# Two attention forms computed by pairs of 64-wide heads, with the values stationary and the output left transposed

## The reference

```python
def one_block(qi):                      # full attention, layers 1 and 2
    s = jnp.einsum("bqgrd,bkgd->bgrqk", qi, k)
    p = jax.nn.softmax(s, axis=-1)
    return jnp.einsum("bgrqk,bkgd->bqgrd", p, v)
...
valid = (jnp.abs(rel) <= WINDOW) & (kpos[:, None, :] >= 0) & (kpos[:, None, :] < S)
scores = jnp.where(valid[None, :, None, None], scores, NEG)   # banded, layers 3 and 4
m = jnp.maximum(jnp.max(scores, axis=-1, keepdims=True), sink_l)
p = jnp.exp(scores - m)
p = p / (jnp.sum(p, axis=-1, keepdims=True) + jnp.exp(sink_l - m))
...
p = jax.nn.softmax(s, axis=-1)          # differential, layers 3 and 4
w = p[:, :, 0] - lam * p[:, :, 1]
...
mixed = jnp.concatenate([attn_out, ssd_out], axis=-1)
x = x + jnp.einsum("ble,ed->bld", mixed, w_out[i])
```

## Time and profile before

| | us |
|---|---|
| median of three runs | 2754.73 |
| the profiled execution, its own time | 2757.43 |
| its span, first to last instruction | 2755.6 |
| TensorE busy, share of the span | 2574.8, 93% |
| VectorE busy | 1522.2, 55% |
| ScalarE busy | 886.4, 32% |
| GpSimd busy | 303.1, 11% |
| mean granted TensorE clock, share of full | 0.956 |

### The profile page before, as it was taken

One profiled execution on the slowest core, in us unless ns is written; L12 is line 12 of the kernel. 1 busy time (PEld: TensorE's weight loads), 2 busy tenths in 40 slices (PEclk: granted clock), 3 DMA queues, 4 the chain that ended last, 5 costly groups with the idle time before them and its releaser, 6 DMA issues.

```text
span 2755.6 us, 31048 instructions
## 1 busy us (share of the span) xinstructions
PE 2574.8 (93%) x12620; PEld 2146.9 (78%) x12620; DVE 1522.2 (55%) x2164; ACT 886.4 (32%) x1284; POOL 303.1 (11%) x205
## 2 busy tenths in 40 slices
PE   7898899999998889999999778999999796999999
PEld 6677788888877778888887667888888585888887
DVE  5755543434575554443467675646465767464645
ACT  4351332223335133222242453322233244322222
POOL 2102200000210120000035101000002600100000
PEclk9999899999999989999999788999999888999999
DMA  4200022222310002222222001222232200132232
GB/s 166 77 16 1 31 97 102 92 96 102 109 63 31 1 31 92 94 105 92 92 95 99 21 1 47 92 94 101 96 107 103 81 1 1 61 107 92 92 107 92
DMA packets 30238, 205.33 MB, mean 75 GB/s; under 512 B 3344, under 2 KB 3728, under 8 KB 6032
## 3 DMA queue, kind: packets, MB, share of 16 engines
q1 hardware_dynamic: 30096, 203.35, 20.8%
HBM read 201.24 MB, written 2.10 MB: 74 GB/s over the span
## 4 chain that ended last, share of the span: by engine, by line
PE 80%; DVE 11%; POOL 3%; ACT 3%; issue 2%; DVEq 1%; ACTq 0%; DMA 0%; SPq 0%; POOLq 0%
PE bank L1304 23%; PE bank L1306 23%; PE bank L1305 23%; PE bank L1416 3%; PE bank L1427 2%; PE bank L1386 1%; POOL b_sqs L1281 1%; POOL head_rs L1285 1%; PE bank L1556 1%; ACT b_p L599 1%; DVE b_p L1157 1%; PE bank L1595 1%; DVE a_conv L867 1%; DVE ssq L698 1%; DVE neg_max L1186 1%
## 5 line engine op out<-in xcount | busy, mean ns | idle before, releaser
L622 DVE TENSOR_TENSOR w_lo<-w_raw,w_hi 128x2048 fp32r<-128x2048 f32 (+1 forms) x190 | 433.9, 2284 | 413.6 <-ACT w_hi L306 413.4
L1304 PE MATMUL bank<-h_ffn_hi,w_hi 128*128 128x512 f32 x1408 | 548.6, 390 | 0.0
L1306 PE MATMUL bank<-h_ffn_hi,w_lo 128*128 128x512 f32 x1408 | 547.8, 389 | 0.0
L1305 PE MATMUL bank<-h_ffn_lo,w_hi 128*128 128x512 f32 x1408 | 547.7, 389 | 0.0
L306 ACT ACTIVATE w_hi<-w_raw 128x2048 fp32r<-128x2048 f32 (+1 forms) x190 | 360.0, 1895 | 558.8 <-PE bank L1306 511.1
L1306 PEld LDWEIGHTS bank<-h_ffn_hi,w_lo 128*128 128x128 f32 x1408 | 264.3, 188 | 55.0
L1305 PEld LDWEIGHTS bank<-h_ffn_lo,w_hi 128*128 128x128 f32 x1408 | 264.3, 188 | 54.8
L1304 PEld LDWEIGHTS bank<-h_ffn_hi,w_hi 128*128 128x128 f32 x1408 | 264.3, 188 | 54.4
L1304 PE MATMUL bank<-act_hi,w_hi 128*128 128x512 f32 x704 | 273.9, 389 | 0.0
L1305 PE MATMUL bank<-act_lo,w_hi 128*128 128x512 f32 x704 | 273.9, 389 | 0.0
L1306 PE MATMUL bank<-act_hi,w_lo 128*128 128x512 f32 x704 | 273.9, 389 | 0.0
(11 more groups left out here) (292 smaller groups left out, 3716.0 us busy)
## 6 DMA issues: line engine op xcount, KB each, us to landing
w_raw<-weights SPq DMA_DIRECT2D x188, 1024.0 KB, 4.7
residual<-x_in SPq DMA_DIRECT2D x8, 256.0 KB, 6.2
x_out<-residual SPq DMA_DIRECT2D x8, 256.0 KB, 2.1
cst<-consts SPq DMA_DIRECT2D x1, 960.0 KB, 10.7
par_b<-params_b SPq DMA_DIRECT2D x1, 627.0 KB, 11.7
par_a<-params_a SPq DMA_DIRECT2D x1, 244.0 KB, 2.7
w_raw<-weights SPq DMA_DIRECT2D x2, 64.0 KB, 1.9
```

The lines of the kernel that those rows point to most:

```text
L622: nc.vector.tensor_tensor(w_lo[s][:, cols], w_raw[s][:, cols], w_hi[s][:, cols].bitcast(F32), ALU.subtract).then_inc(w_ready, 1)
L1304: mm(out, ahi, bhi, start=start, stop=False)
L1305: mm(out, ahi, blo, start=False, stop=False)
L1306: return mm(out, alo, bhi, start=False, stop=stop)
```

## The change

Heads are taken by twos. A key tile is no longer copied into two half-empty ones: head 2j uses rows 0 to 63 of query and key tile and head 2j + 1 rows 64 to 127, each with its own bank (`S_BANKS`). The masks of the banded part come behind the scores and only for the outer blocks. The turned probabilities stream while 64 columns of v are stationary, one head giving partitions 0 to 63 and the other 64 to 127 of bank 4, so that the output is transposed. The reciprocals of the sums are spread over the partitions by eight small products (bank 3), copied, multiplied in (`normalise`), and the result is split where it lies (`out_hi`, `out_lo`): no transposes for these four tiles, which `w_out` takes first, with the turns of the other four behind its first twelve matmuls. Transposes follow the scores two units later instead of one, and VectorE takes the maxima of a differential unit ahead of the weights of the one before. SyncE, GpSimd and the DMAs have the same instructions. Parts of the diff:

```diff
-            def key_hi(m, base, dst):
-                act.wait_ge(t_done, base + m + 1)
-                for half in range(2):
-                    last = nc.scalar.activation(dst[:, key_tile(m, half), :], bank[5 + m % 2][:, :], ACT.Identity,
-                                                scale=half_mask[:, half:half + 1])
-                last.then_inc(t_hi_done, 1)
...
+            def pair_exp(lay, i, par_, width, probs):
+                act.wait_ge(max_done, 32 * lay + 2 * i + par_ + 1)
                 if i >= 2:
+                    act.wait_ge(pt_done, 32 * lay + 2 * (i - 2) + par_ + 1)
+                c = 2 * i + par_
+                nc.scalar.activation(probs[i % 2][par_][:, 0:width], bank[S_BANKS[i % 2][par_]][:, 0:width], ACT.Exp,
+                                     bias=neg_max[:, c:c + 1], accum_out=denom[:, c:c + 1]).then_inc(e_done, 1)
...
+            def normalise(lay, t, r_sb, on):
+                dve.wait_ge(r_taken, 4 * lay + t + 1)
+                dve.wait_ge(o_done, 32 * lay + 8 * t + 8)
+                nc.vector.tensor_tensor(on[:, :], bank[4][:, :], r_sb[:, :], ALU.mult).then_inc(o_free, 1)
+            def out_lo(lay, t, on, hi, lo):
+                dve.wait_ge(o_hi_done, 4 * lay + t + 1)
+                ts_ = slice(t * P, (t + 1) * P)
+                nc.vector.tensor_tensor(lo[:, :, ts_], on[:, :].rearrange("p (j q) -> p j q", q=P), hi[:, :, ts_].bitcast(F32),
+                                        ALU.subtract).then_inc(o_ready, 1)
...
+                    for par_ in range(2):
+                        c = 2 * i + par_
+                        dve.wait_ge(s_done, base + c + 1)
+                        nc.vector.tensor_reduce(neg_max[:, c:c + 1], bank[S_BANKS[i % 2][par_]][:, 0:window(i // 4)[1] * P],
+                                                AX.X, ALU.max, negate=True)
                     dve.drain()
-                    nc.vector.tensor_scalar(neg_max[:, i:i + 1], recip[:, i:i + 1], par[:, B_SINK + h:B_SINK + h + 1], -1.0,
-                                            ALU.max, ALU.mult).then_inc(max_done, 1)
+                    j = i % 4
+                    nc.vector.tensor_tensor(neg_max[:, 2 * i:2 * i + 2], neg_max[:, 2 * i:2 * i + 2], neg_sink[:, 2 * j:2 * j + 2],
+                                            ALU.min).then_inc(max_done, 2)
...
-                for i in range(16 + 4):
+                for i in range(20):
+                    if i < 16:
+                        diff_max(i)
+                    if i == 0:
+                        out_lo(lay, 3, B["b_on"], B["b_ot_hi"], B["b_ot_lo"])
                     if 1 <= i <= 16:
-                        diff_weights(i - 1)
-                    if i < 16:
-                        for c in range(2):
-                            dve.wait_ge(ds_done, 32 * l + 2 * i + c + 1)
-                            nc.vector.tensor_reduce(neg_max[:, 2 * i + c:2 * i + c + 1], bank[(5, 6, 1, 2)[2 * (i % 2) + c]][:, :],
-                                                    AX.X, ALU.max, negate=True).then_inc(dmax_done, 1)
-                    if i >= 7 and (i - 3) % 4 == 0:
-                        t = (i - 3) // 4 - 1
+                        diff_coef(i - 1)
+                    if i >= 7 and i % 4 == 3:
+                        t = (i - 7) // 4
                         take_diff(t)
                         if t >= 1:
...
+            def pair_attention(lay, windows, q_of, k_of, v_of, masked, probs, pts, between):
+                base = 32 * lay
+                def blocks(u):
+                    return window(u // 4) if windows else (0, TB)
+                for i in range(19):
                     if i in between:
                         between[i]()
+                    if i < 16:
+                        t, j = divmod(i, 4)
+                        k0, nb = blocks(i)
                         if i >= 2:
+                            pe.wait_ge(e_done, base + 2 * (i - 2) + 2)
                         qs, ks = slice(t * P, (t + 1) * P), slice(k0 * P, (k0 + nb) * P)
+                        qh, ql = q_of(j)
+                        for n in range(3):
+                            for par_ in range(2):
+                                rows = slice(par_ * HD, (par_ + 1) * HD)
+                                kh, kl = k_of((j // 2) ^ par_)
+                                q_, k_ = ((qh, kh), (qh, kl), (ql, kh))[n]
+                                last = mm(bank[S_BANKS[i % 2][par_]][:, 0:nb * P], q_[rows, qs], k_[rows, ks],
+                                          start=(n == 0), stop=(n == 2 and not masked))
+                                if n == 2 and not masked:
+                                    last.then_inc(s_done, 1)
+                        if masked:
+                            for par_ in range(2):
+                                outer = [b for b in range(nb) if k0 + b != t]
+                                for b in outer:
+                                    last = mm(bank[S_BANKS[i % 2][par_]][:, b * P:(b + 1) * P], id_bf[:, :], mask_bf[:, k0 + b - t + 1, :],
+                                              start=False, stop=(b == outer[-1]))
+                                last.then_inc(s_done, 1)
+                    if 2 <= i < 18:
+                        u = i - 2
+                        nb = blocks(u)[1]
+                        for par_ in range(2):
+                            pe.wait_ge(e_done, base + 2 * u + par_ + 1)
+                            if u >= 1:
+                                pe.wait_ge(ptc[par_], 16 * lay + u)
+                            for b in range(nb):
+                                last = nc.tensor.transpose(bank[PT_BANKS[par_]][:, b * P:(b + 1) * P],
+                                                           probs[u % 2][par_][:, b * P:(b + 1) * P], ident)
+                            last.then_inc(pt_done, 1)
+                    if i >= 5 and i % 4 == 1:
+                        t = (i - 5) // 4
+                        pe.wait_ge(recip_ready, 4 * lay + t + 1)
+                        if t >= 1:
+                            pe.wait_ge(r_taken, 4 * lay + t)
+                        for j in range(4):
+                            for par_ in range(2):
+                                c = 8 * t + 2 * j + par_
+                                last = mm(bank[3][par_ * HD:(par_ + 1) * HD, j * P:(j + 1) * P],
+                                          recip[:, c:c + 1].to_broadcast([P, HD]), ident, start=True, stop=True)
+                        last.then_inc(r_done, 1)
                     if i >= 3:
+                        u = i - 3
+                        t, j = divmod(u, 4)
+                        k0, nb = blocks(u)
+                        if j == 0 and t >= 1:
+                            pe.wait_ge(o_free, 4 * lay + t)
+                        for par_ in range(2):
+                            pe.wait_ge(ptc[par_], 16 * lay + u + 1)
                         for b in range(nb):
+                            for par_ in range(2):
+                                last = mm(bank[4][par_ * HD:(par_ + 1) * HD, j * P:(j + 1) * P], v_of(j // 2, k0 + b),
+                                          pts[u % 2][par_][:, b * P:(b + 1) * P], start=(b == 0), stop=(b == nb - 1))
+                                if b == nb - 1:
+                                    last.then_inc(o_done, 1)
...
-            def w_out(g0, base, n):
+            def w_out(lay, g0, base, n, ot_hi, ot_lo, src):
                 for g in range(g0, g0 + QUARTERS):
                     enter(g)
                     for half in range(2):
                         j = 2 * (g % 2) + half
                         open_bank(j, g)
+                        if g == g0 and half == 0:
+                            pe.wait_ge(o_ready, 4 * lay + 4)
                         for k in range(KT):
-                            if g == g0 and half == 0:
-                                pe.wait_ge(t_free, base + n + k + 1)
+                            if g == g0 and half == 0 and k == 4:
+                                pe.wait_ge(mix_ready, lay + 1)
+                                for m in range(4):
+                                    turn(n + m, base, lambda t: src[:, t, m * P:(m + 1) * P])
+                            if g == g0 and half == 0 and k >= 4:
+                                pe.wait_ge(t_free, base + n + k - 4 + 1)
                             ws = slice(k * COLS + half * P, k * COLS + half * P + P)
-                            last = three(bank[j][:, :], w_hi[g % 2][:, ws], w_lo[g % 2][:, ws], h_mix_hi[:, k, :], h_mix_lo[:, k, :],
+                            hi, lo = (ot_hi, ot_lo) if k < 4 else (h_mix_hi, h_mix_lo)
+                            last = three(bank[j][:, :], w_hi[g % 2][:, ws], w_lo[g % 2][:, ws], hi[:, k, :], lo[:, k, :],
                                          k == 0, k == KT - 1)
...
-                for m in range(8):
-                    if m == 4:
-                        pe.wait_ge(mix_ready, lay + 1)
```

(58 more changed lines are left out.)

345 lines of the change are left out of this document (156 added, 189 removed).

## The result

| | before | after |
|---|---|---|
| median of four runs each, us | 2753.61 | 2665.05 |
| range of the runs | 2751.8 to 2761.34 | 2662.83 to 2666.91 |
| span of the profiled execution | 2755.6 | 2661.0 |
| mean granted TensorE clock | 0.956 | 0.968 |

The ratio is 0.967, 95% interval 0.965 to 0.969: faster by 88.6 us in the medians, 94.6 in the profiled spans. The forecast was 66 less (2688.5); the direction was right and the result lies inside the range of 2655 to 2748, in its lower part.

A forecast was written before the change was run, and what follows sets the result against it. TensorE was taken to bound the kernel, except VectorE's waits in the differential part. Two layers at -18.6 and two at -14.6 gave -66 us: 2691 from the profile's 2757.4, 2688.5 from the median; range 2655 to 2748.

The forecast's parts named there:

- Column halves, x = 0.055: Value and reciprocal products: x, the price of one column-half instruction, is 0.055 us, two halves going side by side.
- Rival A: Column-half products: the halves take turns, x = 0.108 us an instruction, +58 us, 2746 in all; chance 0.17.
- rival C: Column-half products: a load waits for the neighbour's streaming, 0.185 us an instruction, +141 us, 2830 in all; chance 0.10.
- The turn, 0.15 each: TensorE in attention pairs: each change of tiling mode costs 0.15 us, three changes a pair.
- less the 0.07 for how the loads fall: Full-attention pair: 0.07 us taken off for how loads fall, bringing the pair from 3.17 to 3.10 us.
- Full attention, -11.4: Full-attention stage: 16 pairs save 13.8 us, less 1.4 at the end and 1 for a later start; -11.4 us a layer.
- The +1.4 at the end: End of full attention: product, ScalarE rounding and VectorE subtraction now stand before the coefficients; +1.4 us.
- Rival B: Attention loops: the handing over between engines binds, 3.5 us a pair instead of 3.1, +26 us, 2714 in all; chance 0.16.
- Banded part, 0: Banded part: pairs at 2.42 us (two blocks) and 3.06 (three), +2.1 - 1.8 over eight of each, so nothing.
- Differential part, -6: Differential part: VectorE's wait for the exponentials is covered, less time given back to TensorE and its low clock; -6 us a layer.
- Output projection, -6 in all four: Output projection: 12 early matmuls -2.8, mixing ending sooner and four turns -2.6, fewer low-clock matmuls -0.6; -6 us a layer.
- Keys, -1.2: Key turns: two copies a turned tile become one on each engine, two tiles; -1.2 us a layer.

The follow-up runs named there:

- the run with short streams: Changed kernel with every value product except the first block's streaming 64 columns instead of 128; 2654.69 us, ratio 0.964.
- the two runs above: Changed kernel, differential part: VectorE's old order alone put back, 2694.03 us (0.978); TensorE's old order alone put back, 2706.89 us (0.983).
- the version with three edits: Changed kernel with differential takings spread, 24 projection matmuls before the mixing wait, full attention's last subtraction behind the first state products; 2646.81 us, ratio 0.961.

## Why the prediction was right

**Column halves, x = 0.055: right.** 0.0575 by the reciprocals, and (1.03 - 0.15) / 16 = 0.055 by the values. Rival A (0.108) and rival C (0.185) fall. The forecast leaned on row halves going in pairs; the run with short streams shows that streaming two at a time sets the pace. That the loads of two column halves overlap is in the trace itself: the sixteen of a pair's values, 0.14 us each, stand within 0.85 us.

```profile
185.06 0.85 PEld L1489 LDWEIGHTS bank<-a_pt,a_v 128*64 128x64 f32 x16 [0.17 <-issue]
```

The rule that stood behind rival C, that a load overlaps only where the row group differs (the Trainium skill, TensorE: Matmul & The Clock Gate, Part 3), would by rival C's estimate of 0.185 have made a pair's values 3 us; the trace disagrees, with 1.03.

**The turn, 0.15 each: right** (0.15 to 0.17). The "less the 0.07 for how the loads fall" was wrong: without it the pair would have come to 3.17, and 3.16 was measured. By the Trainium skill (TensorEngine Tiling (Array Packing), Key Properties) a change of mode drains the engine; the pair of 3.30 instead of 2.95 us in the run with two more turns agrees.

**Full attention, -11.4: nearly right**, -12.2. Two terms erred and offset each other: the pairs gave 16 x 0.80 = 12.8 instead of 13.8, and the start and the interruptions, priced at +1, cost 0.8 less than before. The +1.4 at the end was there, as moving the subtraction showed. Rival B fell: pairs start every 2.95 us without a gap, and no handing over binds the loop.

**Banded part, 0: wrong, -4.3 beyond the entry.** The step that failed is "scores are held by their loads, two of 128 columns a pass at 0.105 each". A two-block and a three-block pair:

```profile
1534.23 0.39 PE L1446 MATMUL bank<-b_kt_hi,h_mix_hi 64*128 64x256 f32 x2
1534.45 0.28 PE L1446 MATMUL bank<-b_kt_lo,h_mix_hi 64*128 64x256 f32 x2
1534.57 0.28 PE L1446 MATMUL bank<-b_kt_hi,h_mix_lo 64*128 64x256 f32 x2
1534.78 0.29 PE L1454 MATMUL bank<-mask_bf,id_bf 128*128 128x128 bf16 x2
1534.90 0.61 PE L1465 MATMUL bank<-cst,b_p 128*128 128x128 f32 x4
```

```profile
1517.44 0.44 PE L1446 MATMUL bank<-b_kt_hi,h_mix_hi 64*128 64x384 f32 x2
...
1518.52 0.84 PE L1465 MATMUL bank<-cst,b_p 128*128 128x128 f32 x6
1519.29 0.88 PE L1489 MATMUL bank<-b_pt,b_va 128*64 128x128 f32 x12
1520.10 0.44 PE L1446 MATMUL bank<-b_kt_hi,h_mix_hi 64*128 64x384 f32 x2
```

The third pass of both heads starts 0.12 after the second, not 0.21 (1534.45 to 1534.57): the loads of two row halves share time as their streams do. The trace has both loads of the third pass in the same 0.19 us (from 1534.45 on). The first pass, behind a change of mode, takes 0.22. Two-block scores with their turn are 0.55, not 0.82, and two masks 0.12, not 0.20. Summed with values at 0.58 and reciprocals at 0.23 a two-block pair is 2.0 (priced 2.42), a three-block one 2.66 + 0.23 = 2.9 (priced 3.06): 8 x 0.42 + 8 x 0.17 = 4.7.

**Differential part, -6: the mechanism right, the size off**, -8.7 and -9.0. The wait of the reciprocal for the exponentials is gone. VectorE's work alone is 2.4 us a unit (2.48 was priced); up to the first taking such units alternate with some of 2.6 to 2.9 (2.62 in the rows below), behind it not, where "two units in 5.14, 2.57 each" was priced throughout. The first taking is 2.4 us (1563.61 to 1566.01) and not 2.99, as it has no scaling. "About 1.5 after each of three" takings was there behind two of them, 1.72 and 1.50; behind the third no maxima follow. That the order is the cause, VectorE's and TensorE's alike, the two runs above show.

```profile
1557.41 0.15 DVE L1188 RECIPROCAL recip<-denom 128x2 f32<-128x2 f32 x1
...
1560.03 0.15 DVE L1188 RECIPROCAL recip<-denom 128x2 f32<-128x2 f32 x1
...
1562.43 0.15 DVE L1188 RECIPROCAL recip<-denom 128x2 f32<-128x2 f32 x1
```

**Output projection, -6 in all four: right in sum** (-8.8, -7.9, -6.4, -3.6, mean -6.7), too small in layers 1 and 2 and too large in 4. "Fewer matmuls at the low clock, -0.6" was the mis-sized term. In the 30 us from the last y or value product on, the mean granted clock of the four layers was 0.83, 0.77, 0.75 and 0.84 before and is 1.00, 0.94, 0.89 and 0.84 after: in the first layer it doesn't fall at all, in the last it is as low as it was, and the savings fall with the difference. The gap in the middle of the first half, forecast as some 4 us, is 2.6 (1.42 and 1.13) in layer 1 and 3.2 (2.03 and 1.13) in layer 3.

**Keys, -1.2: right in layers 1 and 2, wrong in 3 and 4** (-3.3, -4.3), and the state-space part, not priced, gave 1.5 and 1.9. What goes beyond the price is clock. In layer 1 the first eight state products take 3.4 us before (219.40 to 222.81) and 1.8 after (205.10 to 206.93). The turns of layer 3, first of the kernel before, then of the changed one (second last columns: PEclk):

```profile
1538.00:1549.40 11.40, 8.73 (x32) 5.52 (x31) 6.23 (x9) 5.13 (x9) 0.00 (x0) 0.50 0.00 0
```

```profile
1490.00:1498.20 8.20, 4.39 (x27) 2.62 (x25) 5.53 (x8) 4.47 (x8) 0.00 (x0) 0.98 0.00 0
```

TensorE reaches 2.4 GHz half-way through the turns; before, it stayed at 1.2 GHz to their end. What TensorE did before that: behind the first key tile it stood still 1.95 us in the kernel before, and 0.56 now that the second copy is gone. That this let the clock rise is argued, not shown by a run. In layer 4 some 2 of the 4.3 us are chance: with the same code there, the turns took 16.3 us in the changed kernel and 18.1 to 18.2 in six of the versions above.

The shortfall of the forecast, 28 us on the profiled runs, is then: banded part 8.6, differential part 5.7, turns 5, state-space part 3.4, projection 2.7, full attention 1.6, start 1.1. The errors all went one way. Half of the shortfall, 14 us, lies in the banded and the differential part, where work and waits were priced too high; 11 lie in the turns, the state-space part and the projection, where the prediction priced little or none of the clock that is won behind a removed gap. That the result still lies in the range is in part luck: its lower bound stood for turns between modes that cost nothing, and they cost what was priced.

## What to carry to other kernels

Two 64-column products with the same rows and different columns of the array cost one, if they alternate; group them, since each change between row halves, column halves and the whole array costs 0.15 to 0.17 us. When an order across engines is changed, price all engines' orders as one and undo none alone. Look for gaps in front of TensorE: the piece of another engine's work that makes one can be spread, or work of TensorE's own can fill it. Here gaps of 2.0, 2.3 and 4.4 us were followed by instructions at the low clock and one of 1.42 was not; filling the gap of 4.4 with 2.8 us of work gave 3.1 to 5.9 us.

## What the hardware showed that was not expected

A column-half product whose neighbour is in the same half costs 0.085, though a product of twice the columns on the whole array takes 0.216; what sets 0.085 stays open.

The state-space part takes 72 us in one execution and 77 to 79 in another, with the same instructions and hardly a difference in front of it. Its stretch from 220 on in the changed kernel, and in the version with three edits, where it begins 1.2 us sooner:

```profile
215.00:220.00 5.00, 0.87 (x5) 0.47 (x4) 4.76 (x8) 0.00 (x0) 0.00 (x0) 1.00 0.00 0
220.00:225.00 5.00, 5.00 (x22) 3.90 (x22) 0.88 (x2) 0.00 (x0) 0.00 (x0) 0.66 0.01 3
225.00:230.00 5.00, 4.43 (x41) 4.25 (x40) 1.97 (x3) 1.19 (x2) 2.08 (x2) 1.00 0.00 0
```

```profile
215.00:220.00 5.00, 1.36 (x2) 0.84 (x3) 4.52 (x8) 0.00 (x0) 0.00 (x0) 0.76 0.00 0
220.00:225.00 5.00, 5.00 (x19) 4.10 (x18) 0.00 (x0) 0.00 (x0) 0.00 (x0) 0.50 0.02 3
225.00:230.00 5.00, 5.00 (x27) 4.68 (x25) 0.69 (x1) 0.60 (x1) 1.04 (x1) 0.50 0.00 0
```

The idle time in front is nearly the same; the clock is back at full by 225 in one, and not yet at 230 in the other. Over the whole part it is 0.88 against 0.82. In the version with three edits this gives back 4.7 of the gain in the first layer and nothing in the second. Full attention of the first layer does the same: 60.3 us in the changed kernel, 63.4 in the version with VectorE's order put back and in the one with both halves of the projection first, with the same code there (clock 0.94 and 0.92). What decides it stays open. Differences of a few us between versions of this kernel can be this and nothing else.
